# Later weight lows in the RWKV stage, and a merge stage in halves of the tokens

## The reference

```
xn = rms_norm(x)                                   # 2048 channels
u  = xn @ w_in                                     # one projection for both mixers and the gates
o_a = rwkv7_mixer(u_a)                             # 16 heads of 64, delta-rule state
o_b = nsa_mixer(u_b) * silu(g_b)                   # compressed + selected + window attention
merged = sig(u_ma) * (o_a @ w_pa) + sig(u_mb) * (o_b @ w_pb)
h = x + merged @ w_o
y = rms_norm(h)                                    # norm_out
```

## Time and profile before

| what | us |
|---|---|
| median of 3 runs (2466.09 to 2470.59) | 2466.56 |
| profiled execution, device time | 2464.72 |
| its span, first to last instruction | 2463.0 |
| TensorE matmul busy | 2261.5 (92%) |
| VectorE, ScalarE, GpSimd busy | 1193.0, 803.2, 532.9 |
| mean granted TensorE clock | 0.967 |

### The profile page before, as it was taken

How to read it: one execution, slowest core, us unless ns; L and a number is a source line. 1 busy time by engine, 2 the same in 40 slices (tenths; PEclk the granted TensorE clock), 3 DMA queues, 4 the chain that set the end, 5 groups by cost and what they waited for, 6 DMA issues and landing times. The chain is left out here.

```text
span 2463.0 us, 51947 instructions
## 1 busy us (share of the span) xinstructions
PE 2261.5 (92%) x21510; PEld 2082.4 (85%) x21510; DVE 1193.0 (48%) x2352; ACT 803.2 (33%) x1593; POOL 532.9 (22%) x398
## 2 busy tenths in 40 slices
PE   5999999899999989999999789899989869999996
PEld 4998888787888878899999778788987669999996
DVE  4343545445454545368887264444226425353223
ACT  4334233332323332222222345455223214232221
POOL 0000000000000000001100699999604420000000
PEclk8999999999999999999999899999989889999998
DMA  3321112212121121288675412321559955443232
GB/s 114 104 88 50 63 52 71 72 42 71 49 68 50 64 84 51 78 269 282 225 245 181 146 61 83 86 65 55 195 185 307 312 170 181 141 139 128 97 100 82
DMA packets 134590, 302.09 MB, mean 123 GB/s; under 512 B 26442, under 2 KB 54324, under 8 KB 132820
## 3 DMA queue, kind: packets, MB, share of 16 engines
q1 hardware_dynamic: 95236, 208.86, 25.7%
q0 software_dynamic: 15824, 54.71, 6.5%
q10 hardware_dynamic: 23296, 35.20, 4.4%
HBM read 261.48 MB, written 45.54 MB: 125 GB/s over the span
## 5 line engine op out<-in xcount | busy, mean ns | idle before, releaser
L178 PE MATMUL acc<-xh,w_hi 128*128 128x272 f32 x3008 | 675.5, 306 | 42.1 <-DVE w_lo L161 17.9
L178 PE MATMUL acc<-xl,w_hi 128*128 128x272 f32 x3008 | 632.1, 292 | 0.0
L178 PE MATMUL acc<-xh,w_lo 128*128 128x272 f32 x3008 | 631.9, 292 | 0.0
L178 PEld LDWEIGHTS acc<-xh,w_hi 128*128 128x128 f32 x3008 | 479.0, 193 | 101.0 <-issue 53.5
L178 PEld LDWEIGHTS acc<-xl,w_hi 128*128 128x128 f32 x3008 | 484.1, 193 | 0.0
L178 PEld LDWEIGHTS acc<-xh,w_lo 128*128 128x128 f32 x3008 | 481.1, 193 | 0.0
L161 DVE TENSOR_TENSOR w_lo<-w_raw,w_hi 128x1024 fp32r<-128x1024 f32 x164 | 200.6, 1223 | 422.0 <-ACT w_hi L153 421.1
L153 ACT ACTIVATE w_hi<-w_raw 128x1024 fp32r<-128x1024 f32 x188 | 198.4, 1055 | 295.3 <-PE acc L178 220.7
L1265 DVE SCALAR_TENSOR_TENSOR b_C<-b_rows,b_pos_s,b_C 128x512 f32<-128x512 f32 x240 | 162.4, 744 | 0.0
L2618 DVE TENSOR_TENSOR m_w_lo<-m_w,m_w_hi 128x1024 fp32r<-128x1024 f32 x64 | 78.4, 1224 | 164.2 <-ACT m_w_hi L2563 164.1
L970 PEld LDWEIGHTS rbank<-m 64*64 64x64 f32 x3840 | 120.2, 135 | 22.9 <-issue 14.1
(11 more groups left out here) (408 smaller groups left out, 3350.4 us busy)
## 6 DMA issues: line engine op xcount, KB each, us to landing
w_raw<-in_w_all SPq DMA_DIRECT2D x168, 512.0 KB, 3.5
b_rows<-in_cmp_rows SPq DMA_DIRECT2D x128, 256.0 KB, 3.8
m_w<-in_w_mo SPq DMA_DIRECT2D x64, 512.0 KB, 3.9
w_raw<-in_w_all ACTq DMA_DIRECT2D x20, 512.0 KB, 5.9
tmp_uT<-ub ACTq DMA_DIRECT2D x35, 272.0 KB, 4.0
m_gates<-tmp_uT SPq DMA_DIRECT2D x32, 272.0 KB, 2.7
d_ring<-in_sel_k SPq DMA_DIRECT2D x64, 128.0 KB, 4.4
d_ring<-in_sel_k POOLq DMA_DIRECT2D x64, 128.0 KB, 4.6
```

The costliest lines, as they stand in the source:

```text
L178: ins = self.nc.tensor.matmul(acc[:, c, 0:HALF], w[:, k % KH, :], x[:, k, c * HALF:(c + 1) * HALF], start=(k == 0 and m == 0), stop=(k == ...
```

## The change

Three things change.

1. RWKV stage: VectorE's `background` takes lows two pieces later (place 4(h-2)+2), four later when it is called ahead of a UV update; and it is called once more, behind each state update with the place of the next U.
2. Sample stage: the last `store` stands ahead of the rest of ScalarE's background.
3. Merge stage. Unit 0 runs column half 0 for all 8 tiles, then turns the samples, then runs column half 1; the prompt's columns of o_a are split without waiting for the samples. In both engines' programs a weight's parts now stand ahead of the tiles 0, 3 and 5. The samples' DMA is issued by ScalarE, not GpSimd. The w_o pass is run twice, for token half 0 and then for token half 1: 32 units of 48 matmuls, every w_o weight loaded and split twice (`N_HALVES` 96, was 64). Residual, square, sum, root, reciprocal, scalings and stores are per token half; those of half 0 stand in units 51 to 59.

```diff
-            def background(upto):
-                while lows[0] < W.h_ahead and HALF_PIECES * (lows[0] - 2) <= upto:
+            def background(upto, late=2):
+                while lows[0] < W.h_ahead and HALF_PIECES * (lows[0] - 2) + late <= upto:
...
                 def got(name):
-                    background(place[i, name])
+                    background(place[i, name], HALF_PIECES if name[0] == "U" else 2)
...
                     last.then_inc(ev_dve, 1)
+                    if n + 1 < NCH:
+                        background(place[i, f"U{n + 1}"])
                     go_on(preparing, AFTER_S[n])
...
+            store(N_BP - 1)
             background(SAMPLE_PIECES)
-            store(N_BP - 1)
...
-        UNITS = 3 * N_OUT
+        UNITS = 4 * N_OUT
+        SCALE_AT = 2 * N_OUT + 20
...
-            act.wait_ge(taken, 1)
             for k in range(KW):
                 if k % 4 == 0:
                     act.wait_ge(oa_in[k // 4], 16)
+                if k in (0, 3, 5):
+                    high_part((k + 1) // 2 - (k > 0))
                 o_high(k)
-                if k in (1, 3, 5):
-                    high_part((k - 1) // 2)
+            act.wait_ge(taken, 1)
+            f(o_hi[:, 0:KW, SEQ:NT], o_raw[:, 0:KW, SEQ:NT], ACT.Copy).then_inc(o_hi_done, 1)
...
+            def inverse(t):
+                cols = slice(t * HALF, (t + 1) * HALF)
+                dve.wait_ge(rooted, t + 1)
+                link(v.reciprocal(prod[:, 1, cols], prod[:, 0, cols]))
+                dve.wait_ge(squared, N_OUT * (t + 1))
...
+                if n == SCALE_AT:
+                    dve.wait_ge(g_out_in, 16)
+                    inverse(0)
+                if SCALE_AT <= n < SCALE_AT + N_OUT // 2:
+                    for k in range(2):
+                        scale(0, 2 * (n - SCALE_AT) + k)
...
+            def first_unit():
+
+                pe.wait_ge(w_lo_done, 1)
+                for c in range(2):
+                    if c:
+                        pe.wait_ge(ident_in, 16)
+                        pe.wait_ge(oa_s_in, 16)
+                        turn_samples(0, oa_s)
+                        pe.wait_ge(o_lo_done, KW + 1)
+                    for k in lower:
+                        if c == 0:
+                            pe.wait_ge(o_lo_done, k + 1)
...
+                    parts = ((n - 2 * N_OUT) // N_OUT,)
+                    ready = (m_lo_done, 0) if n == 2 * N_OUT else None
+                    half(x, out, lower, m_hi, m_lo, True, False, ready, parts)
+                    half(x + 1, out, upper, m_hi, m_lo, False, True, ready, parts)
```

More of the change, by code:

```diff
@@ L2530, in _ @@
                     residuals[0] += 1
-            for c in range(residuals[0], N_OUT):
+            for c in range(residuals[0], 2 * N_OUT):
                 sp.wait_ge(added, c - 1)
@@ L2547, in _ @@
             nc.gpsimd.memset(ones[:, :], 1.0).then_inc(ones_set, 1)
[L2548 to L2551, removed]
+            for t in range(2):
+                cols = slice(t * HALF, (t + 1) * HALF)
+                for q in range(4):
+                    pool.wait_ge(scaled, N_OUT * t + 4 * q + 4)
+                    pool.dma_start(A["yT"][:, 4 * q:4 * q + 4, cols], h[:, 4 * q:4 * q + 4, cols]).then_inc(sent, 16)
+            pool.wait_ge(sent, 128)
         @block.scalar
@@ L2569, in o_high, with square, root @@
             def o_high(k):
[L2570 to L2576, removed]
-            act.wait_ge(taken, 1)
+                cols = slice(0, SEQ if k < KW else NT)
+                f(o_hi[:, k, cols], o_raw[:, k, cols], ACT.Copy).then_inc(o_hi_done, 1)
+            def square(u):
+                t, c = divmod(u, N_OUT)
+                act.wait_ge(added, u + 1)
+                if u >= 2:
+                    act.wait_ge(summed, u - 1)
+                f(sq[:, u % 2, 0:HALF], h[:, c, t * HALF:(t + 1) * HALF], ACT.Square).then_inc(squared, 1)
+            def root(t):
+                act.wait_ge(summed, N_OUT * (t + 1))
+                act.wait_ge(m_lo_done, N_OUT)
+                f(prod[:, 0, t * HALF:(t + 1) * HALF], sum_sq[:, t, 0:HALF], ACT.Sqrt, bias=eps[:, 0:1], scale=1.0 / D_MODEL)\
+                    .then_inc(rooted, 1)
             for k in range(KW):
@@ L2602, in _ @@
                     square(n - 1 - 2 * N_OUT)
-            square(N_OUT - 1)
-            act.wait_ge(summed, N_OUT)
-            f(two(prod[:, 0, :]), sum_sq[:, :, 0:HALF], ACT.Sqrt, bias=eps[:, 0:1], scale=1.0 / D_MODEL).then_inc(rooted, 1)
+                if n == SCALE_AT - 1:
+                    root(0)
+            square(2 * N_OUT - 1)
+            root(1)
         @block.vector
@@ L2661, in finish @@
                     add_residual(n)
+            for k in range(KW):
+                if k in (0, 3, 5):
+                    low_part((k + 1) // 2 - (k > 0))
+                o_low(k)
             dve.wait_ge(tps, 1)
             v.tensor_copy(o_raw[:, 0:KW, SEQ:NT], turn[0][:, 0:KW * NS].rearrange("p (k n) -> p k n", n=NS)).then_inc(taken, 1)
[L2664 to L2667, removed]
+            dve.wait_ge(o_hi_done, KW + 1)
+            v.tensor_tensor(o_lo[:, 0:KW, SEQ:NT], o_raw[:, 0:KW, SEQ:NT], o_hi[:, 0:KW, SEQ:NT].bitcast(F32), ALU.subtract)\
+                .then_inc(o_lo_done, 1)
             for n in range(UNITS):
@@ L2713, in turn_prompt, with half @@
                 ins.then_inc(tps, 1)
-            def half(x, out, tiles, x_hi, x_lo, start, stop, ready):
+            def half(x, out, tiles, x_hi, x_lo, start, stop, ready, parts=(0, 1)):
                 pe.wait_ge(w_lo_done, x + 1)
@@ L2725, in half, with square_sum @@
                 ins.then_inc(half_done, 1)
[L2727 to L2733, removed]
-            lower, upper = range(KW), range(KW, KD)
-            pe.wait_ge(ident_in, 16)
-            pe.wait_ge(oa_s_in, 16)
-            turn_samples(0, oa_s)
+            def square_sum(u):
+                pe.wait_ge(squared, u + 1)
+                t, c = divmod(u, N_OUT)
+                mm(sum_sq[:, t, 0:HALF], ones[:, :], sq[:, u % 2, 0:HALF], start=(c == 0), stop=(c == N_OUT - 1))\
+                    .then_inc(summed, 1)
+            lower, upper = range(KW), range(KW, KD)
+            def first_unit():
[9 more added lines that the diff above has]
+                            pe.wait_ge(o_lo_done, k + 1)
+                        for m, (a, b) in enumerate(((w_hi, o_hi), (w_hi, o_lo), (w_lo, o_hi))):
+                            ins = mm(acc[0][:, c, 0:HALF], a[0][:, k, :], b[:, k, c * HALF:(c + 1) * HALF],
+                                     start=(k == 0 and m == 0), stop=(k == KW - 1 and m == 2))
+                ins.then_inc(half_done, 1)
             for n in range(UNITS):
```

61 lines of the change are left out of this document (33 added, 28 removed).

## The result

| what | before | after |
|---|---|---|
| median of the timed runs, us | 2467.49 (4 runs, 2466.09 to 2470.59) | 2412.90 (4 runs, 2409.68 to 2415.71) |
| profiled execution: device time, span | 2464.72, 2463.0 | 2411.98, 2410.3 |
| TensorE matmul busy | 2261.5 (92%) | 2253.5 (93%) |
| mean granted clock | 0.967 | 0.971 |

The ratio is 0.978, with a 95% interval of 0.9768 to 0.9792. The span fell by 52.7 us, where 58.8 was forecast. The two traces part it like this; the ends of the stretches are the last matmul pair of the RWKV stage (1027.53, now 972.67), the first DMA of the merge (2014.63, now 1960.61), the start of the first product of unit 3 and the end of the last one of the w_o pass.

The account below looks back on a forecast made before the run. TensorE, busy 92% of the span, was taken as the bound, losing time to waits and a lowered clock. Terms -37.8 - 5.3 - 12.2 - 0.2 + 5.6 - 8.9 = -58.8 us gave 2407.8 us, own range 2400 to 2422, overall 2398 to 2431.

Parts of the forecast that it names:

- UV waits: RWKV stage: the S job's waits for VectorE's UV update fall from 42.5 to 4.7 us, ten left; 37.8 us go.
- State update's wait: RWKV stage: the U job of chunk 1 no longer waits for the first state update; 5.3 us go.
- The clock: RWKV stage: the granted clock no longer falls at or behind the waits; 12.2 us go, 4 us as low end.
- the row's 0.45: TensorE's clock: each us at the lower level loses 0.45 us, from matmuls 0.45 us apart there, 0.249 at full clock.
- What a later low costs: RWKV stage: lows taken two to four pieces later leave over 4 us of slack; cost taken as nothing.
- The rival of the pile-up: RWKV stage: lows delay prepared work, so half of the UV wait and clock loss return; 2435 us, chance 0.14.
- Merge's start: Merge, unit 0 to unit 3: tiles stand behind weight 1; 8.4 us lost, net 5.6, with ends of 4.0 and 11.
- The rival in which the first product pays double: Merge's start: weight 1 lands later than now and the clock stays low through unit 1; 2418 us, chance 0.10.
- w_o pass: Merge: same matmuls, now consecutively into one PSUM bank; 0 taken, between 0 and 51 us.
- the rival of the slow weights: Merge's w_o pass: weights come too slowly, 85 us more there; 2493 us, slower than before, chance 0.04.
- The end: Merge, last matmul to span's end: halved columns and no table load there save 8.9 us, between 7.5 and 10.
- Sample stage: Sample stage: the last attention store is issued earlier, the projection's store still bounds the barrier; 0.2 us gained.

Follow-up runs that it names:

- the time alone changed: The changed kernel without the extra call behind each state update, lows still two or four pieces later: 2410.76 us, ratio 0.9776 to the kernel before.
- the place alone changed: The changed kernel with the extra call behind each state update, but every low at the old time: 2495.88 us, ratio 1.0123 to the kernel before.
- that experiment: The changed kernel with the low at each pair's chunk 3 U job taken at the old time again: 2442.09 us, ratio 0.9903 to the kernel before.

## Why the prediction held, and where it did not

The forecast was 2407.8 us, with 2400 to 2422 as its own range; 2412.9 us were measured. The mechanism in the RWKV stage was right. The five stretches together came out 6.1 us worse than their sum, each a little, and 2.7 of it at the merge's start.

**UV waits, -37.8 forecast, -37.3 measured.** The count of ten remaining waits was exact, their mean 0.52 us where 0.47 was taken. The reason holds, but it is narrower than I put it. I had argued from the place of the low in the order (and three lows of the last pair do stand directly ahead of UV). The experiments say that what counts is that the high is done when VectorE reaches the low. With the time alone changed the waits go; with the place alone changed they grow to 58.5 us.

**State update's wait, -5.3.** Gone, as forecast. It stays at 5.3 us where the lows keep their old time.

**The clock, -12.2.** From the first to the last S job 56.3 us went. The waits are 42.6 of them; 13.7 are left for the clock, 1.5 more than the forecast. The experiment with one low put back makes the term shown and not only argued: 10.5 us beyond its waits, 10.7 by the row's 0.45. Ahead of every fall in the scans TensorE had stood for UV. In the kernel before and with one low of each pair put back, all nine waits of 3.0 us or more were followed by a fall, but only four of the eight of 2.5 to 2.6 us. The seventeen waits of up to 1.04 us with every low one piece later were followed by none. With the place alone changed, three waits of 1.75 us were followed by a fall and four of 2.0 us were not. So the length of a wait does not settle it alone, and what else does stays open. By the Trainium skill's statement that the clock has two levels only ("TensorE: Matmul & The Clock Gate", Part 1), a shortfall of 1.19 windows is 23.8 us at the lower one; the trace agrees, since at 0.45 us lost per us that makes 10.7 us, within 0.2 of what the stretch was longer by beyond its waits.

**What a later low costs, 0.** Nearly: one low came 2.09 us late, at 160.00, before the scans; my slack of over 4 us was wrong at that one place. The scans began 1.5 us later than before (first S job at 227.60, not 226.09), which just cancels the 1.5 us that the clock gave beyond its forecast: that the stage as a whole came within 0.4 us of its -55.3 is in part luck. The rival of the pile-up did not come: no S or U job waited for prepared work.

**Merge's start, +5.6 forecast, +8.3 measured.** The steps on the way were right: TensorE began 11.8 us in (12.2 forecast), weight 1 stood among the tiles, the gap was 5.81 us, and the wait ahead of unit 3 went. What failed is the term "I take full" for column half 1. The clock was still low and half 1 took 5.3 us, not 3.0; that is 2.3 of the missing 2.7 us. The bound of 11 us had it. What I did not see is that the order itself was avoidable: with the weights behind the tiles the column halves cost little or nothing. The rival in which the first product pays double did not come: the high of weight 1 began 17.0 us into the stage, 16.9 before, so moving the samples' DMA to the other engine brought it no earlier, and the clock was up from unit 1 on. Its sum was also wrong: 6 us at 0.45 make 2.7 us, not 5.4.

**w_o pass, 0 forecast.** From its first to its last product it took 206.97 us, 204.38 before. The units of token half 0 repeat every 6.51 us and those of half 1 every 6.47, against 12.88 for a pair of before; that is 0.14 and 0.06 us a pair, and the rest lies at the pass's ends. If all of it were the one-bank order, which no run isolates, 2.6 us over 1536 matmuls are 0.0017 us each, near the lower end of my bounds of 0 and 0.033. Units 3 to 31 gave 1.3 us back, with the clock up where it had been 0.87 in the 10 us behind the start of unit 3 (2057 to 2067). So +1.3 in sum. The weights were no trouble: loads landed in a median of 3.8 us, and no product waited for one. The pass moved 179 GB/s, not the 230 that I had counted in the rival of the slow weights.

**The end, -8.9 forecast, -8.4 measured.** Every row came within 0.06 us of its term but the square sum, 0.73 for 0.5; from the last scaling to the end it took 4.6 us where it had been 5.5, 0.2 less gain than I had counted. The Trainium skill ("ScalarE: Activation LUTs", What ACT_TABLE_LOAD costs) counts 1283 ns for a load and a drain of 1380 ns with it. The load is 1.28 us in both traces, but no drain shows on either side of it: in the earlier trace rows the square ends at 2440.65, the load stands from 2440.66 to 2441.94 and the root begins at 2441.96. Nor did the load cost its whole length, for the square sum's matmuls ran beside it. Their row, which belongs to the earlier trace rows:

```profile
2440.70 1.19 PE L2731 MATMUL m_sum_sq<-m_sq,m_ones 128*128 128x272 f32 x4 [0.59 <-ACT m_sq L2576]
```

They ended at 2441.89, so without the load the root could have started at most 0.07 us sooner. From the end of the square to the start of the root it took 1.31 us before and 0.81 after. This 0.5 us, where I had counted 0.78, needed both edits, the load gone and the square sum halved; either one alone would have left the root waiting for the other.

**Sample stage, -0.2 forecast.** The stretch of attention and samples varied between 983.9 and 990.6 us over the ten other profiled executions, in which little or nothing was changed there; so neither -0.2 nor the measured +0.8 can be told, and no run tests the moved store by itself.

## What to carry to other kernels

When an engine takes its instructions in order, background work must not be issued at the moment its input is released, but when its input is surely there: a low two pieces later cost next to nothing, a low at the first possible moment made the chained step behind it wait for an evacuation, a high and a low. Count a standstill of TensorE of 2.5 to 3.1 us as here twice, once for the wait and once for the clock that can fall behind it. And when a first unit is to start early, look at each instruction among its inputs that waits for a later load; one such weight took the whole gain of the early start and more.

## What the hardware did that I had not expected

- One wait of 3.10 us in an otherwise unbroken stream of matmuls was followed by a clock of 0.69 over the next ten us, the stream running on. At the eight places of that experiment the clock cost 10.5 us, 1.3 us a wait on average, or 1.75 us for each of its six falls.
- In another experiment the clock fell behind three waits of only 1.75 us, and not behind four of 2.0 us.
- A table load of 1.28 us ran beside the matmuls whose sum the next activation needed, and cost next to nothing there.
- At the merge's start the same program had its clock back up to 10 us earlier or later (0.75 and 0.83 against 0.50 and 0.55 in two windows). A forecast there needs both ends.
- Turning the samples needs the identity matrix, a DMA of 64 KB issued 0.4 us into the stage beside the big loads; TensorE got it only 9.2 us into the stage where the samples were turned first.
